# A transformer layer on one core: operand tiles split per row tile, row sums on VectorE, memory output in two pairs of banks, lagged row steps

## What is computed

```python
y = swiglu(rms_norm(x, g_ff1_pre), w_ff1_gate, w_ff1_up, w_ff1_down)
x = x + 0.5 * rms_norm(y, g_ff1_post)
y = hybrid_mixer(rms_norm(x, g_mix_pre), ...)          # attention with forget gates, gated linear attention
x = x + rms_norm(y, g_mix_post)
y = memory_cross_attention(rms_norm(x, g_mem_pre), rms_norm(mem, g_mem_src), ...)
x = x + rms_norm(y, g_mem_post)
y = swiglu(rms_norm(x, g_ff2_pre), w_ff2_gate, w_ff2_up, w_ff2_down)
x = x + 0.5 * rms_norm(y, g_ff2_post)
out = rms_norm(x, g_final)
```

## Time and profile before

| | us |
|---|---|
| median of 3 runs | 2526.53 |
| lowest, highest | 2521.24, 2567.23 |
| the profiled execution | 2527.4 |
| its span (first to last instruction) | 2525.7 |
| TensorE busy in it | 2304.9 (91%) |
| VectorE, ScalarE, GpSimd busy | 1068.4, 774.0, 587.4 |
| mean granted TensorE clock, share of full | 0.952 |

### The profile page before, as it was taken

One profiled execution on the slowest core, in us unless ns is written; L12 is line 12 of the kernel. 1 busy time (PEld: TensorE's weight loads), 2 busy tenths in 40 slices (PEclk: granted clock), 3 DMA queues, 4 the chain that ended last, 5 costly groups with the idle time before them and its releaser, 6 DMA issues.

```text
span 2525.7 us, 26973 instructions
## 1 busy us (share of the span) xinstructions
PE 2304.9 (91%) x10640; PEld 1870.4 (74%) x10640; DVE 1068.4 (42%) x1276; ACT 774.0 (31%) x1218; POOL 587.4 (23%) x511
## 2 busy tenths in 40 slices
PE   3899999999987999999989799978499999999994
PEld 2788888788865777778767687756378888878884
DVE  5544444464444344451234343232644444454444
ACT  5333333321122433331212243232433333332112
POOL 4343443200032000000144300012534344320005
PEclk7899999999998999999997999989699999999997
DMA  3222222333321000011221241032022222243323
GB/s 108 67 85 82 84 82 86 117 126 99 126 77 58 20 18 18 18 43 42 82 77 51 91 151 42 9 117 67 17 78 90 67 88 96 67 144 115 109 67 117
DMA packets 104958, 195.45 MB, mean 77 GB/s; under 512 B 6993, under 2 KB 72546, under 8 KB 102018
## 3 DMA queue, kind: packets, MB, share of 16 engines
q1 hardware_dynamic: 104834, 193.73, 23.7%
HBM read 153.80 MB, written 39.91 MB: 77 GB/s over the span
## 4 chain that ended last, share of the span: by engine, by line
PE 43%; issue 43%; POOL 6%; DVE 5%; POOLq 2%; ACT 1%; DMA 0%; DVEq 0%; SPq 0%; ACTq 0%
PE ps L1272 10%; PE ps L1274 10%; PE ps L1273 10%; PE ps L1290 3%; PE ps L1292 3%; PE ps L1291 3%; PE ps L1310 2%; POOL x_ring L621 2%; DVE xc L1757 1%; PE ps L1312 1%; PE ps L1311 1%; POOL y L621 1%; DVE x_ring L1717 1%; POOL rs L615 1%; POOLq L723 1%
## 5 line engine op out<-in xcount | busy, mean ns | idle before, releaser
L1272 PE MATMUL ps<-xc,wg 128*128 128x512 f32 x1232 | 485.6, 394 | 65.9 <-ACT fork L837 49.2
L1273 PE MATMUL ps<-xc,wg 128*128 128x512 f32 x1232 | 484.4, 393 | 0.0
L1274 PE MATMUL ps<-xc,wg 128*128 128x512 f32 x1232 | 484.2, 393 | 0.0
L1272 PEld LDWEIGHTS ps<-xc,wg 128*128 128x128 f32 x1232 | 234.2, 190 | 117.9 <-issue 59.5
L1290 PE MATMUL ps<-d_w,d_hid 128*128 128x512 f32 x704 | 276.9, 393 | 7.7 <-DVE y L1795 7.1
L1291 PE MATMUL ps<-d_w,d_hid 128*128 128x512 f32 x704 | 275.6, 392 | 0.0
L1292 PE MATMUL ps<-d_w,d_hid 128*128 128x512 f32 x704 | 275.6, 391 | 0.0
L1274 PEld LDWEIGHTS ps<-xc,wg 128*128 128x128 f32 x1232 | 234.3, 190 | 49.1
L1273 PEld LDWEIGHTS ps<-xc,wg 128*128 128x128 f32 x1232 | 234.3, 190 | 48.9
L1762 DVE TENSOR_TENSOR wg<-w_sums,wg 128x1024 fp32r<-128x1024 f32 x88 | 125.6, 1429 | 200.4 <-ACT wg L831 200.4
L1798 DVE TENSOR_TENSOR y<-y,ps 128x1024 f32<-128x1024 f32 x88 | 107.3, 1220 | 206.5 <-PE ps L1292 206.5
(11 more groups left out here) (259 smaller groups left out, 3947.1 us busy)
## 6 DMA issues: line engine op xcount, KB each, us to landing
w_raw<-in_w_ff_gate SPq DMA_DIRECT2D x22, 1024.0 KB, 6.6
w_raw<-in_w_ff_up SPq DMA_DIRECT2D x22, 1024.0 KB, 5.4
hid_dram<-hid SPq DMA_DIRECT2D x22, 1024.0 KB, 4.6
raw<-hid_dram SPq DMA_DIRECT2D x44, 512.0 KB, 3.8
raw<-in_w_ff_down SPq DMA_DIRECT2D x44, 512.0 KB, 3.7
raw<-in_w_mix_in SPq DMA_DIRECT2D x24, 512.0 KB, 3.9
x_row<-x_dram SPq DMA_DIRECT2D x24, 512.0 KB, 4.1
x_dram<-x_ring SPq DMA_DIRECT2D x16, 512.0 KB, 5.0
```

The costliest lines, as they stand in the source:

```text
L1272: mm(acc, hi, x_hi, start=STARTS[q] and k == 0, stop=False, skip_group_check=True)
L1273: mm(acc, hi, x_lo, start=False, stop=False, skip_group_check=True)
L1274: last = mm(acc, lo, x_hi, start=False, stop=k == 3, skip_group_check=True)
```

## The change

- Operands of the FFs are summed and split per row tile j (all four 128-row blocks of an operand's tile, 128x512 elements an instruction as before) and no longer per 128-row block, so a tile can be split as soon as it is transposed. ScalarE and VectorE have merged orders for it at the start and at the second FF's entry. All sums of operands and of weight group 0 are now VectorE's; GpSimd's are gone. T3 is made as T2 - B11.
- T2 has its own tile, which lies in `w_raw[1]`'s place. So the up weights of group 1 (`load_weights(f, 1)`) are loaded only when the last late sum (T4, tile 3) and T2's split are done.
- fork_off(f, 0, 0) stands ahead of the operands that come late; `high_w(f, 1, 0)` and fork_off(f, 0, 1) stand in their old order.
- `add_row` becomes VectorE's second instruction in `scale_y`, at boundaries 1 to 4.
- In `ff_2` scale_y, make_row, high_h, low_h and keep_v come one step later each.
- The memory output projection uses banks 4, 5 for even tiles and 2, 3 for odd ones, and waits for the scaling two tiles back.
- The four turn_mem come behind mq(0, 1); ScalarE and VectorE have the matching order.
- At the start x's tiles lie in six buffers instead of eight, the first is loaded ahead of the gain, and the last two wait for a buffer.

The diff, cut to its core:

```diff
@@ tiles and counts
-        xs = {q: at_kb(f"xs{q}", 16 * q + 8, [P, 4, HT]) for q in (OP_T1, OP_T3, OP_T4)}
+        xs = {q: at_kb(f"xs{q}", 16 * q + 8, [P, 4, HT]) for q in (OP_T3, OP_T4)}
+        xs[OP_T2] = at_kb("xs2", 156, [P, 4, HT])
-        x_first = at_kb("x_first", 80, [P, NT, D])
+        x_first = [at_kb(f"x_first{i}", 80 + 4 * (i % 6), [P, D]) for i in range(NT)]
...
+        X_ALL = [[(q, j) for j in range(4) for q in (OP_B11, OP_B21)] + [(q, j) for j in range(4) for q in (OP_T2, OP_T1)],
+                 [(q, j) for q in (OP_B11, OP_B21, OP_T2, OP_T1) for j in range(4)]]
+        X_COUNT = [{e: 28 * f + n + 1 for n, e in enumerate(X_ALL[f] + [(q, j) for q in (OP_T3, OP_B22, OP_T4) for j in range(4)])}
+                   for f in range(2)]
+
+        def x_src(q, j):
+            if q in xs:
+                return xs[q][:, :, tile_of(j)]
+            rows, i = {OP_B11: (0, j), OP_B21: (4, j), OP_T1: (0, 4 + j), OP_B22: (4, 4 + j)}[q]
+            return h_all[:, rows:rows + 4, tile_of(i)]
...
-        OUT_BANK = 4
+
+        def out_bank(bd, i):
+            return 2 if bd == 3 and i % 2 else 4
+
@@ SyncE: ff_loads; the start; before the second FF
             def ff_loads(f):
+                sp.wait_ge(x_summed_late, 8 * f + 8)
+                sp.wait_ge(xc_lo_done, X_COUNT[f][OP_T2, 3])
+                load_weights(f, 1)
                 for m in range(NM):
...
-            load_gains(0)
-            for i in range(4):
-                sp.dma_start(x_first[:, i, :], x[0][tile_of(i), :]).then_inc(x_in[i], 16)
-            load_weights(0, 0)
-            for i in range(4, NT):
-                sp.dma_start(x_first[:, i, :], x[0][tile_of(i), :]).then_inc(x_in[i], 16)
-            load_weights(0, 1)
+            for i in range(NT):
+                if i == 1:
+                    load_gains(0)
+                if i == 4:
+                    load_weights(0, 0)
+                if i >= 6:
+                    sp.wait_ge(h_row_done, i - 5)
+                sp.dma_start(x_first[i][:, :], x[0][tile_of(i), :]).then_inc(x_in[i], 16)
...
-            for m in range(2):
-                load_weights(1, m)
+            load_weights(1, 0)
@@ GpSimd: add_row and sum_x(f) gone, with sum_weights(f, 0); order in ff_2
-            def add_row(bd, i):
-                pool.wait_ge(x_row_in[i % 2], 16 * (before(bd, i) // 2 + 1))
-                pool.wait_ge(t1_done, before(bd, i) + 1)
-                new = x_new_of(bd, i)
-                gp.tensor_tensor(new, new, rows_of(bd)[i % 2][:, :], ALU.add).then_inc(x_new_done, 1)
...
                 for s in range(NT):
+                    root1(bd, s)
                     if s > 0:
                         root2(bd, s - 1)
-                    root1(bd, s)
-                    add_row(bd, s)
...
-            for i in range(4):
+            for i in range(NT):
                 root2(0, i)
-            sum_weights(0, 0)
-            for i in range(4, NT):
-                root2(0, i)
-            sum_x(0)
@@ ScalarE: ff_1, end of ff_2
             def ff_1(f):
-                for g in (1, 2):
-                    high_w(f, 0, g)
-                for q in (OP_T2, OP_T1, OP_T3, OP_B22, OP_T4):
-                    for k in range(4):
-                        high_x(f, q, k)
+                high_w(f, 0, 2)
+                for q in (OP_T3, OP_B22, OP_T4):
+                    for j in range(4):
+                        high_x(f, q, j)
                 for m in range(NM):
                     gate, nxt = m % 2 == 0, m + 1 < NM
                     if not gate:
                         silu(f, m // 2, 3)
                     high_w(f, m, 3)
-                    fork_off(f, m, 0)
+                    if m > 0:
+                        fork_off(f, m, 0)
                     if nxt:
                         high_w(f, m + 1, 0)
...
-                for s in range(NT + 2):
+                for s in range(NT + 3):
                     if s < NT:
                         square1(bd, s)
                     if 0 < s <= NT:
                         square2(bd, s - 1)
+                    if f == 0 and s >= 4:
+                        keep_v(s - 4)
                     if f == 0 and s >= 3:
-                        keep_v(s - 3)
-                    if f == 0 and s >= 2:
-                        high_h(bd, s - 2)
+                        high_h(bd, s - 3)
@@ ScalarE: the start; memory; the second FF's entry
+            for i in range(NT):
+                if i < NT - 1 and i != 3:
+                    square2(0, i + 1)
+                keep_h(0, i)
+                if i == NT - 1:
+                    fork_off(0, 0, 0)
+                for q in (OP_B11, OP_B21) if i < 4 else (OP_T2, OP_T1):
+                    high_x(0, q, i % 4)
+                if i == 3:
+                    high_w(0, 0, 0)
+                    square2(0, i + 1)
+                if i == 6:
+                    high_w(0, 0, 1)
+            act.wait_ge(sq2_done, NT)
...
+            high_h(2, NT - 1)
+            for c in range(2):
+                keep_mq(c, 0, c)
             for j in range(2):
                 square_mem(j)
...
+            high_s(S_MK)
+            keep_mq(0, 1, 2)
+            for b in range(4):
+                high_mem(b)
+            high_s(S_MK + 1)
+            keep_mq(1, 1, 3)
...
-                if i == 5:
+                if i == 6:
                     high_w(1, 0, 0)
-                if i in (6, 7):
                     act.wait_ge(mo_lo, NT)
-                    for k in range(4):
-                        high_x(1, (OP_B11, OP_B21)[i - 6], k)
+                    for q in (OP_B11, OP_B21):
+                        for j in range(4):
+                            high_x(1, q, j)
+            for j in range(3):
+                high_x(1, OP_T2, j)
             keep_h(1, NT - 1)
-            for i in (6, 7):
-                act.wait_ge(x_sent[i], 48)
+            fork_off(1, 0, 0)
+            high_w(1, 0, 1)
+            high_x(1, OP_T2, 3)
+            for j in range(4):
+                high_x(1, OP_T1, j)
@@ TensorE: wait of the first products; out_tile; the start; memory
+                if m == 0:
+                    pe.wait_ge(xc_lo_done, X_COUNT[f][q, 3])
                 for k in range(4):
-                    if m == 0:
-                        pe.wait_ge(xc_lo_done, 28 * f + 4 * q + k + 1)
...
-                wait(pe, t1_done, 8 * (bd - 1) + i)
+                if bd == 2 or i < 2:
+                    wait(pe, t1_done, 8 * (bd - 1) + (i if bd == 2 else 0))
+                else:
+                    pe.wait_ge(t1_done, before(bd, i - 2) + 1)
...
-            for i in range(5):
+            for i in range(4):
                 turn(0, i)
             ff_product(0, 0, P1)
-            turn(0, 5)
-            turn(0, 6)
             ff_product(0, 0, P2)
-            turn(0, 7)
+            for i in range(4, NT):
+                turn(0, i)
...
                 mq(c, 0, c)
             turn(2, NT - 1)
-            for b in range(2):
-                turn_mem(b)
             mq(0, 1, 2)
-            for b in range(2, 4):
+            for b in range(4):
                 turn_mem(b)
             mq(1, 1, 3)
@@ VectorE: scale_y; the sums and splits of the operands
                 ve.scalar_tensor_tensor(out=x_new_of(bd, i), in0=src, scalar=rs1[:, i:i + 1], in1=gb_of(bd)[:, 0, :],
                                         op0=ALU.mult, op1=ALU.mult).then_inc(t1_done, 1)
+                dve.wait_ge(x_row_in[i % 2], 16 * (before(bd, i) // 2 + 1))
+                dve.wait_ge(t1_done, before(bd, i) + 1)
+                ve.tensor_tensor(x_new_of(bd, i), x_new_of(bd, i), rows_of(bd)[i % 2][:, :], ALU.add).then_inc(x_new_done, 1)
...
+            def sum_x(f, j):
+                dve.wait_ge(h_all_done, 16 * f + 2 * j + 10)
+                one = x_src(OP_T1, j)
+                ve.tensor_tensor(one, one, x_src(OP_B11, j), ALU.subtract).then_inc(x_summed, 1)
+                dve.wait_ge(x_summed, 8 * f + 2 * j + 1)
+                ve.tensor_tensor(x_src(OP_T2, j), x_src(OP_B22, j), one, ALU.subtract).then_inc(x_summed, 1)
+
+            def sum_x_late(f, q, j):
+                dve.wait_ge(x_summed, 8 * f + 2 * j + 2)
+                if f == 1:
+                    dve.wait_ge(rows_done, 2 * NT)
+                else:
+                    dve.wait_ge(h_row_done, NT)
+                two = x_src(OP_T2, j)
+                if q == OP_T3:
+                    op = ve.tensor_tensor(x_src(q, j), two, x_src(OP_B11, j), ALU.subtract)
+                else:
+                    op = ve.tensor_tensor(x_src(q, j), x_src(OP_B21, j), two, ALU.subtract)
+                op.then_inc(x_summed_late, 1)
...
+            def sum_first_weights(f):
...
+            def low_x(f, q, j):
+                dve.wait_ge(xc_hi_done, X_COUNT[f][q, j])
+                ve.tensor_tensor(xc[:, q, 1, :, tile_of(j)], x_src(q, j), f32(xc[:, q, 0, :, tile_of(j)]),
```

(62 more changed lines are left out.)

## The result

| | before | after |
|---|---|---|
| median us (runs) | 2546.88 (4) | 2434.76 (4) |
| lowest, highest | 2521.24, 2567.94 | 2432.62, 2449.73 |
| ratio, 95% interval | | 0.966 (0.9592 to 0.9727) |
| span of the profiled execution | 2525.7 | 2430.8 |
| TensorE busy, granted clock | 2304.9, 0.952 | 2286.2, 0.969 |

What follows compares the result with a forecast made beforehand. The prediction took TensorE as the bound, with losses between products, in the tail and in slow-clock stretches. Its terms summed to 89.4 us, taken from the profiled 2527.4 to give 2438 us, range 2420 to 2462.

Steps and rivals of the forecast that it cites:

- terms 7: Last turn to P7, both FFs: fork wait replaced by one behind a late load; -3.7 us first, -5.7 second.
- term 5: Memory output: separate banks remove the scaled-row wait, tiles every 11.8 us instead of 15.8; -26.4 us.
- rival (a): FF entries give nothing as the late load takes 12 us, other terms fall short; 2471 us, chance 0.11.
- Term 1: Tail behind the last matmul: VectorE's step falls to 4.9 to 5.0 us, under TensorE's 5.44; -17.6 us.
- Rival (b): Row loops: VectorE becomes the bound with an add of 2.4 to 3.3 us; 2464 us, chance 0.07.
- Term 2: Boundary 1: value steps shorten as rows come earlier and GpSimd's add stops delaying make_row; -14 us.
- Term 3: Mixer output: the new row and next norm come 1.2 us earlier, some waits shrink; -4.5 us.
- Terms 4 and 6: Start of the memory branch, queries ahead of memory rows: -8 us; to the last turn before the second FF: -9.5.
- What was costed at nothing: Six x buffers, group 0 weight sums on VectorE, odd memory tiles' banks, old-row loads, keep_v's wait: no cost claimed.
- (c): Reordering fails since turn(3, i-1) or low_h becomes the next wait at once; 2480 us, chance 0.08.
- (d): Slower: TensorE stays at 1.2 GHz through the output tiles and boundary 1; 2582 us, chance 0.04.

Runs made afterwards that it cites:

- The run with the rows alone: Kernel before plus only the old-row adds on VectorE and the one-step lag in the last down groups, engine orders matched: 2484.49 us for 2527.39.
- the run with one pair: Changed kernel with the memory output projection back in one pair of banks, each tile waiting for the scaling of the tile before: 2463.47 us.

## Why the prediction was right, point by point

- **The sum.** Nine places, each within 2 us of its term. The gain in the profiles is 5.5 us more than predicted. 3.0 of it are in the two terms 7. The prediction charged 0.9 us at each FF for slow matmuls behind P7, and the stretch from the second P7 to the last matmul is no longer than before (653.8 for 654.0). P7 does start slowly in the kernel after, nine matmuls 0.4 us apart from 1762.22; but it was so in the kernel before too, where eight were so from 1840.89, and the prediction set nothing against its charge. Two small slips of its arithmetic: the parts of term 5 add up to 26.3 and those of P7's 29.8 to 29.7. The first entry ran 0.9 us ahead of the steps worked out at each of them (turn(0, 4) at 32.31 for 33.2, load issued at 64.05 for 64.8, P7 at 73.18 for 74.1).
- **Terms 7, the new wait.** Right in kind, size and cause, shown by two runs: bring the load forward and P7 follows, take the fork out of its way and P7 starts without it. The load took 5.4 and 5.5 us; rival (a) wanted 12. What ended the old wait for fork 0 is not shown in parts: the splits by tile, the fork's earlier place and the sums on VectorE were never undone one by one. The run with the rows alone shows only that none of the gain there comes from the rows.
- **Term 1.** Its size was right (the last row starts 10.4 us behind the last matmul; 10.0 was worked out) and so was the step, but the prediction treated the lag and the engine as one edit. The runs show that each is worth less than half of the gain without the other. Rival (b) needed an add of 2.4 us or more on VectorE; it takes 1.2.
- **Term 2.** 14.7 for 14. The steps with a unit take 9.3 us (9.0 worked out) and the last ones 10.9 with a gap of 2.72. Undoing the lag alone gives back 5.9 us here (turn(1, 7) at 799.61 for 793.70), with the adds on GpSimd 12.8. Of these 9.0 stand at turn(1, 1) already, with scalings of 3.0 to 3.4 us beside an add. Behind it VectorE's scalings take 1.28 us again; there ScalarE's square waits for the add and stands ahead of keep_v and high_h, so that high_h starts 2.7 us behind a turn (754.22 for 751.47) where it was 0.7 (733.79 for 733.10).
- **Term 5.** 27.4 for 26.4. That a quarter of it is clock and not wait was in the sum (1.6 us in four tiles, 6.4 in all); the run with one pair shows 8.2 of 28.2.
- **Term 3** was short by 1.9, 1.1 of which lies ahead of the loop, among the same instructions. Terms 4 and 6 are right to 0.7; in the run with lag and GpSimd's adds the mixer output takes 143.8 us from turn(2, 0) to turn(2, 7), 138.6 in the kernel after and 143.2 before, so that part of term 3 is the add's move.
- **What was costed at nothing** cost nothing: no TensorE wait is put down to x, an old row or a free bank. No row speaks for rivals (c) and (d): no new wait took over at once except the one forecast, and the clock rose from 0.952 to 0.969.

## What to carry to other kernels

When a stall ends, go down the queue of the instruction that it held and ask what is late next, DMAs too: the load that nobody waited for before was the next wait, and in the run that freed P7 the one after that, a fork of the next group, took 3.4 us of the gain at the second FF. Price an edit in two parts as two edits: a lag that lets an engine run ahead brings little while that engine's step is still too long for another reason. When a time comes out as expected, look whether it did so in the place that was changed. Give an add to the engine that reads the same rows next, rather than to a free one that runs beside it, when the row of the page shows a 1.28 us instruction at 3.4.

## What the runs showed of the hardware that was not expected

A stretch of small matmuls runs at either level of the clock in executions of near the same program. The stretch behind the forget gates, in the kernel after and in the run without the lag (as above):

```profile
853.90:886.90 33.00, 32.45 (x211) 24.53 (x212) 22.64 (x52) 14.36 (x35) 0.00 (x0) 1.00 0.12 33
```

```profile
859.00:892.00 33.00, 32.62 (x116) 24.07 (x116) 14.90 (x31) 10.01 (x24) 0.00 (x0) 0.54 0.11 32
```

TensorE is busy for 32.5 and 32.6 us of them, with no wait longer than 0.8, but gets through 211 matmuls in the one and 116 in the other. Between turn(1, 7) and the output loop the second kernel loses 13.5 us (461.5 for 448.0), most of the 21 by which it missed its expectation. Executions of one kernel differ by as much, with the mean clock: the kernel after has one of 2449.73 us (0.962) beside three of 2432.6 to 2435.2 (0.966 to 0.969), the run without the lag one of 2449.97 (0.963) beside three of about 2465 (0.958 to 0.960). The run with lag and GpSimd's adds has the same stretch in its profiled execution (2484.26) and not, by their times, in the other three (2470.9 to 2472.3), so its miss of 27 is tail (26.4 for 12 to 13) and boundary 1. What comes before the stretch differs: in the kernel after the clock had last been down at 817 to 824 us, in the other at 803 to 807. What decides it was not tried and stays open; a gain under 15 us in the mixer can be read only from places with the same clock.
